# Expert stage of a diffusion step on one core: turns joined, weight rows paired, more buffers, last product reordered

## The chip, the core and the metric

One core of a Trainium2 chip runs the whole program. The metric is the device time of one launch in microseconds, taken several times; the profile is one further execution, recorded by the hardware profiler.

## What is computed

One layer of a hybrid backbone in float32: 128 context tokens and 512 latent tokens, each of 1,024 features. A mixer (a gated linear recurrence and differential attention behind one input projection) is followed by a mixture of 16 experts. Each expert chooses its tokens itself, 64 latent and 16 context ones, so that it always works on 80 rows:

```
aff = softmax(h @ router_w); gate, idx = top_k(aff per expert, cap)      # cap 64 latent, 16 context
xg = h[idx]                                                              # gathered rows
a = silu(xg @ w_gate[e]) * (xg @ w_up[e])
y = (a @ w_down[e]) * gate
x = x + g2 * scatter_add(y at idx)
```

h is the normalised x, scaled and shifted by a modulation that is itself a product of a conditioning vector with w_mod. The three weight matrices of an expert are 1,024 x 1,024 each, 4 MiB; all experts together are 192 MiB, and each is read once.

## The kernel before, in words

There is one instruction stream for each engine, written out by hand. The order of the first part comes from a list STEPS that all engines walk through; the expert stage has loops of its own. Waits are on semaphores.

**Ahead of the experts.** Weights come in pieces of 1 MiB or less through three raw buffers, are split by ACT (L959) and DVE (L1186) into a high and a low part (w_hi, w_lo), and the activations lie split in act_hi and act_lo. The small inputs are loaded by SP at L760 between the pieces, five of them on the semaphore s_late, for which DVE (L1366) and PE (L1812, L1838) wait. After the output projection each token tile is normalised to xn2, written to a DRAM tensor xn_rows (SP, L840), turned by PE with eight transposes (L1982) for the router, and the residual is written to the output (SP, L834). Then DVE picks the tokens of all experts, PE makes the rows of the second modulation (L1725, L1792, L1793), and GpSimd starts the first indirect gather.

**Experts on PE.** The weights of an expert are 12 pieces of 1 MiB (gate 4, up 4, down 4), each two blocks of 128 input features by 1,024 outputs; a piece's two blocks are its two "halves". piece_mm (L2030) takes one piece: for each half it runs four matmuls at L2037 for the latent rows (stationary operand 128 x 32 tokens, moving 512 columns, into four 32-partition strips of one PSUM bank) and four at L2040 for the context rows (256 columns each). The trace lists each float32 matmul as two. The order on PE for expert e is gate(e), up(e), down(e-1). turn_x(e+1) (L2017, L2020) stands in the middle of up(e): eight transposes that bring the 80 gathered rows xg into the layout features by tokens, into PSUM pair 3. turn_a(e) (L2044, L2047) stands at the end: six transposes of the hidden activations aa, into the same pair. The last down product has no other work beside it and is done in the same order, piece by piece (L2089).

**Experts on the other engines.** DVE: xmod (L1645, L1647) scales and shifts the turned tokens into xT; hidden (L1652) multiplies silu(gate) by up; yout (L1661 for the latent rows, L1666 for the context rows) scales the down product into ye. ACT: silu (L1159) and the copy of the turned activations to hT (L1161). GpSimd: an indirect gather (L906) for each expert from xn_rows into the one buffer xg, and two indirect scatters with addition (L922 for the latent rows, L925 for the context rows) into the outputs; at the end of each scatter it waits until both have landed.

**Weights in the expert stage.** SP issues the 192 pieces at L823 into a ring of NRE = 14 buffers. Fourteen pieces come as buffers fall free from the first part: piece 0 early, 1 to 4 when the last projection is done, 5 to 8 around the last rows of the outputs (L841 to L844), 9 and 10 after the first gather has landed (L848), 11 to 13 when the last modulation pieces are used. From then on piece n waits at L853 for PE to be done with piece n - 14. act_hi and act_lo lie idle in the expert stage.

The diff touches these functions:

Of the kernel before, what the change touches and what calls it, by code (L numbers as in the profile page):

```python
# [39 lines left out]
def fused_step(nc, A, outs):  # L40
# [8 lines left out]
    with ExitStack() as ctx:  # L49
# [169 lines left out]
        NRE, NP = 14, 12 * NE  # L219
# [12 lines left out]
        Wraw = [[ctx.enter_context(nc.sbuf_tensor(f"w_raw{v}{s}", [P, 2048], F32))[:, :] for s in range(NHL)] for v in range(2)]  # L232
        brow = arena[:, o_vso + 2048:o_vso + 2560]
# [11 lines left out]
        xpsum = pair(3).rearrange("p (k t) -> p k t", k=KD)[:, :, 0:CAP]  # L245
# [374 lines left out]
        s_silu, s_a, s_aT, s_ahi, s_y, s_yc, s_scat = (sem(n) for n in ("s_silu", "s_a", "s_aT", "s_ahi", "s_y", "s_yc", "s_scat"))  # L620
# [13 lines left out]
        eraw = [Wraw[1][last_w[0]]] + [Wraw[v][s] for s in last_w[1:] for v in range(2)] + eraw_x  # L634
# [92 lines left out]
        def _(sp):  # L727
# [30 lines left out]

            def load_small(dst, src, sig):
                sp.dma_start(dst, src).then_inc(sig, 16)  # L760
# [16 lines left out]
            for dst, src in small[2:]:  # L777
                load_small(dst, src, s_late)
            STORES = {("gl", 3): range(0, 4), ("gl", 4): range(4, 8), ("f", 0): range(8, 12), ("q", 0): range(12, 16), ("gl", 5): range(16, 20),
                      ("mod", 6, 0): (20, 21), ("mod", 6, 1): (22, 23), ("mod", 7, 0): (24, 25, 26), ("gl", 7): (27,), ("mod", 4, 0): range(28, 32)}  # L780
            out_at = {"nk": RAWNO[("tok", 3, 1)], "nv": RAWNO[("tok", 4, 1)]}
            for n in range(9, len(PIECES)):
# [23 lines left out]
                if n == RAWNO[("out", 1, 0)]:  # L806
# [4 lines left out]
                    sp.dma_start(router, A["router_w"][0].rearrange("(k p) e -> p k e", p=P)).then_inc(s_x1in, 16)  # L811
            wg, wu, wd = (A[n][0] for n in ("w_exp_gate", "w_exp_up", "w_exp_down"))

            def epiece(n):
# [7 lines left out]
                src = w[ex, 2 * P * k:2 * P * k + 2 * P, :].rearrange("(k p) n -> p k n", p=P)  # L822
                sp.dma_start(eraw[n % NRE].rearrange("p (k n) -> p k n", k=2), src).then_inc(s_er[n % NRE], 16)  # L823
# [39 lines left out]
        def _(pool):  # L863
# [52 lines left out]
            def scatter(e):  # L916
                g.tensor_copy(iscat[0:CAP_LAT, 0:1], iS[0:CAP_LAT, e:e + 1]).then_inc(s_icq, 1)
# [1252 lines left out]
```

## Time and profile before

| | us |
|---|---|
| median of 3 runs | 1274.31 |
| lowest, highest | 1273.91, 1276.9 |
| profiled execution, its own time | 1280.71 |
| its span, first to last instruction | 1278.8 |
| PE busy in the span | 1182.0 |
| DVE, ACT, POOL busy | 569.9, 353.5, 137.2 |

PE is the matmuls, PEld the loads of stationary operands, POOL is GpSimd, SP the engine that issues most DMAs (SPq its queue). Matmuls are pipelined and their ends modelled, so that a busy PE need not be at its peak. Rows of the timeline merge instructions of one line that follow each other closely.

### The profile page before, as it was taken

To read this page: it belongs to the slowest core of one execution; us is meant where nothing else is said; L and a number is where in the kernel's file an instruction comes from. 1 tells how busy PE (TensorE), PEld (TensorE's weight loads), DVE (VectorE), ACT (ScalarE), POOL (GpSimd) and SP (SyncE) were. 2 spreads that over 40 slices of the span, in tenths; PEclk is the share of its full clock that TensorE was granted. 3 is DMA by queue.
4 is the path that set the end of the run, shared out by engine and by line. 5 is a ranking of instruction groups with operands and counts; after the bars stand their busy time and mean duration, and the time that the engine had idled before them with its cause. 6 is when DMAs were issued, how large, how long until landed. Compare 5 with 4: busy or idle time off the path is not lost.

```text
span 1278.8 us, 24225 instructions
## 1 busy us (share of the span) xinstructions
PE 1182.0 (92%) x10653; PEld 776.5 (61%) x10653; DVE 569.9 (45%) x833; ACT 353.5 (28%) x561; POOL 137.2 (11%) x192
## 2 busy tenths in 40 slices
PE   5789999999998979679899799999999999999996
PEld 2577888888888868579777434444444444444442
DVE  2787343656268778888875610111111111111112
ACT  3312324555358577554231210000000000000000
POOL 1022000121000101100001000111111111111001
PEclk7889999999999899979999689999999999999999
DMA  8620630311314212206555899999999999999994
GB/s 317 227 97 2 227 101 16 93 43 60 104 44 121 81 60 100 81 18 261 175 172 214 312 347 393 392 390 390 391 391 392 391 391 391 392 394 392 393 400 128
DMA packets 111904, 296.81 MB, mean 232 GB/s; under 512 B 7092, under 2 KB 33076, under 8 KB 111800
## 3 DMA queue, kind: packets, MB, share of 16 engines
q1 hardware_dynamic: 108280, 284.25, 59.0%
q0 software_dynamic: 3520, 11.01, 3.7%
q8 instruction: 84, 1.38, 0.5%
q14 instruction: 20, 0.16, 0.0%
HBM read 278.47 MB, written 16.78 MB: 231 GB/s over the span
## 4 chain that ended last, share of the span: by engine, by line
PE 47%; DVE 2%; ACT 1%; issue 0%; DMA 0%; POOL 0%; POOLq 0%; DVEq 0%; ACTq 0%
PE ps L2037 26%; PE ps L2040 13%; PE ps L1693 1%; PE ps L1695 1%; PE ps L1694 1%; PE ps L2047 1%; PE ps L2020 1%; DVE arena L1310 1%; PE ps L1725 1%; PE ps L1995 1%; PE ps L1982 0%; DMA arena<-in_w_out_dram 0%; ACT w_hi L959 0%; DVE w_lo L1186 0%; DVE arena L1565 0%
## 5 line engine op out<-in xcount | busy, mean ns | idle before, releaser
L2037 PE MATMUL ps<-arena 128*32 128x512 f32 x1952 | 254.5, 593 | 0.9 <-ACT arena L1161 0.9
L1693 PE MATMUL ps<-act_hi,w_hi 128*128 128x320 f32 x576 | 184.7, 321 | 5.2 <-DVE w_lo L1186 2.1
L1695 PE MATMUL ps<-act_hi,w_lo 128*128 128x320 f32 x576 | 179.5, 312 | 0.0
L1694 PE MATMUL ps<-act_lo,w_hi 128*128 128x320 f32 x576 | 179.5, 312 | 0.0
L2040 PEld LDWEIGHTS ps<-arena 128*32 128x32 f32 x1952 | 63.4, 110 | 146.0 <-issue 146.0
L2040 PE MATMUL ps<-arena 128*32 128x256 f32 x1952 | 150.0, 379 | 0.0
L2037 PE MATMUL ps<-w_raw,arena 128*32 128x512 f32 x1120 | 147.8, 600 | 1.4 <-DVE arena L1678 1.4
L1693 PE MATMUL ps<-w_hi,act_hi 128*128 128x512 f32 x280 | 113.7, 406 | 11.8 <-DVE w_lo L1186 4.9
L1693 PEld LDWEIGHTS ps<-act_hi,w_hi 128*128 128x128 f32 x576 | 109.7, 191 | 8.6 <-issue 2.9
L1695 PE MATMUL ps<-w_hi,act_lo 128*128 128x512 f32 x280 | 110.8, 396 | 0.0
L1694 PE MATMUL ps<-w_lo,act_hi 128*128 128x512 f32 x280 | 110.7, 395 | 0.0
L1694 PEld LDWEIGHTS ps<-act_lo,w_hi 128*128 128x128 f32 x576 | 109.7, 190 | 0.0
L1695 PEld LDWEIGHTS ps<-act_hi,w_lo 128*128 128x128 f32 x576 | 109.7, 190 | 0.0
L1645 DVE TENSOR_TENSOR arena<-ps,arena 128x640 f32<-128x640 f32 x15 | 12.4, 824 | 210.6 <-PE ps L2020 210.6
L1161 ACT ACTIVATE arena<-ps 128x768 f32<-128x768 f32 x16 | 13.0, 810 | 337.1 <-PE ps L2047 337.1
L1186 DVE TENSOR_TENSOR w_lo<-arena,w_hi 128x2048 fp32r<-128x2048 f32 (+1 forms) x34 | 73.6, 2166 | 56.3 <-ACT w_hi L959 55.6
L1661 DVE SCALAR_TENSOR_TENSOR arena<-ps,arena 64x512 f32<-64x512 f32 x32 | 23.9, 748 | 148.4 <-PE ps L2040 148.2
L2040 PEld LDWEIGHTS ps<-w_raw,arena 128*32 128x32 f32 x1120 | 36.5, 111 | 85.4 <-issue 85.4
L2037 PEld LDWEIGHTS ps<-arena 128*32 128x32 f32 x1952 | 61.5, 110 | 42.1 <-issue 1.5
L2040 PE MATMUL ps<-w_raw,arena 128*32 128x256 f32 x1120 | 86.7, 382 | 0.0
L963 ACT ACTIVATE arena<-ps 128x512 f32<-128x512 f32 (+2 forms) x80 | 48.4, 617 | 111.4 <-PE ps L1832 27.8
L959 ACT ACTIVATE w_hi<-arena 128x2048 fp32r<-128x2048 f32 (+1 forms) x34 | 61.3, 1808 | 53.4 <-PE ps L1695 24.6
(221 smaller groups left out, 1464.4 us busy)
## 6 DMA issues: line engine op xcount, KB each, us to landing
arena<-in_w_exp_up_dram SPq DMA_DIRECT2D x41, 1024.0 KB
arena<-in_w_exp_down_dram SPq DMA_DIRECT2D x41, 1024.0 KB
arena<-in_w_exp_gate_dram SPq DMA_DIRECT2D x40, 1024.0 KB
w_raw<-in_w_exp_gate_dram SPq DMA_DIRECT2D x24, 1024.0 KB
w_raw<-in_w_exp_up_dram SPq DMA_DIRECT2D x23, 1024.0 KB
w_raw<-in_w_exp_down_dram SPq DMA_DIRECT2D x23, 1024.0 KB
arena<-in_w_mod_dram SPq DMA_DIRECT2D x22, 1024.0 KB, 5.3
arena<-in_w_in_dram SPq DMA_DIRECT2D x18, 1024.0 KB, 6.4
```

Of the source, the lines that this page charges most:

```text
L959: a.activation(hl(key)[0][:, 0:w], rawv(key)[:, 0:w], ACT.Copy).then_inc(s_hi, 1)
L963: release(a.activation(dst, src, func, **kw), key)
L1161: a.activation(hT, pair(3)[:, 0:HW], ACT.Copy).then_inc(s_ahi, 1)
L1186: v.tensor_tensor(l_[:, 0:w], rawv(key)[:, 0:w], h_[:, 0:w].bitcast(F32), ALU.subtract).then_inc(s_lo, 1)
L1310: ins = v.scalar_tensor_tensor(out=out, in0=w[:, kk, :], scalar=by, in1=out, op0=ALU.mult, op1=ALU.add)
L1661: ins = v.scalar_tensor_tensor(out=ye[lat, to], in0=y[64 * b:64 * b + 64, 0:512], scalar=gT[lat, e:e + 1], in1=G2[lat, to], op0=ALU.mult, ...
L1693: t.matmul(out, sh, mh, start=start, stop=False)
L1694: t.matmul(out, sh, ml, start=False, stop=False)
L1695: return t.matmul(out, sl, mh, start=False, stop=stop)
L1725: ins = t.matmul(bank(2 * modpair(j))[32 * kk:32 * kk + 32, :], cond_row[:, 2 * kt:2 * kt + 32], w[:, kk, :], start=s == 0, stop=s == 1)
L2037: t.matmul(bank(2 * pr)[32 * s:32 * s + 32, :], lat[:, 32 * (s % 2):32 * (s % 2) + 32], w[:, kk, 512 * (s // 2):512 * (s // 2) + 512], sta ...
L2040: ins = t.matmul(bank(2 * pr + 1)[32 * s:32 * s + 32, 0:256], ctx_, w[:, kk, 256 * s:256 * s + 256], start=kt == 0, stop=kt == 7)
```

## The change

Five edits come together. The tokens of expert e+2 are turned directly behind the activations of expert e, into PSUM pair 1 (from e = 1 on; the first three turns stay where they were), and the gathers are issued one expert further ahead. The weight pieces are read with two neighbouring rows of the matrix in each partition, so that one partition reads 8,192 bytes in one run; everything that meets those weights follows that order of features: the transposes of x, a and xn2 take every second column, the modulation columns of the second half and their small inputs are paired too, the latter by eight loads of single elements at the start. The ring has 19 buffers, the five new ones (Araw) in the room of act_hi and act_lo, and SP's first pieces are issued in another order. The last down product does the latent rows of all four pieces first, then the context rows. DVE works off yout before the xmod of the expert after next.

```diff
-        NRE, NP = 14, 12 * NE
+        NRE, NP = 19, 12 * NE
+        Araw = [ctx.enter_context(nc.sbuf_tensor(f"a_raw{s}", [P, 2048], F32))[:, :] for s in range(2 * KD * T // 2048)]
-        xpsum = pair(3).rearrange("p (k t) -> p k t", k=KD)[:, :, 0:CAP]
+        def xpair(e):
+            return 3 if e < 3 else 1
+        def xpsum(e):
+            return pair(xpair(e)).rearrange("p (k t) -> p k t", k=KD)[:, :, 0:CAP]
+        def paired(k):
+            return slice(2 * P * (k // 2) + k % 2, 2 * P * (k // 2) + 2 * P, 2)
...
-        eraw = [Wraw[1][last_w[0]]] + [Wraw[v][s] for s in last_w[1:] for v in range(2)] + eraw_x
+        eraw = [Wraw[1][last_w[0]]] + [Wraw[v][s] for s in last_w[1:] for v in range(2)] + Araw + eraw_x
...
 # SP
+            def load_second():
+                sp.wait_ge(s_small, 32)
+                c = A["cols"].rearrange("(p k) n -> p k n", k=2)
+                for h, r in enumerate(HALF):
+                    for dst, c0, n in ((n2c, 8, 8), (bcol[:, 24:40], 56, 16)):
+                        for k in range(2):
+                            with nc.allow_non_contiguous_dma("pairs of features"):
+                                sp.dma_start(dst[r, k::2], c[:, k, c0 + h:c0 + n:2]).then_inc(s_late, 16)
...
             for dst, src in small[2:]:
                 load_small(dst, src, s_late)
+            load_second()
...
-                src = w[ex, 2 * P * k:2 * P * k + 2 * P, :].rearrange("(k p) n -> p k n", p=P)
-                sp.dma_start(eraw[n % NRE].rearrange("p (k n) -> p k n", k=2), src).then_inc(s_er[n % NRE], 16)
+                src = w[ex, 2 * P * k:2 * P * k + 2 * P, :].rearrange("(p k) n -> p (k n)", k=2)
+                sp.dma_start(eraw[n % NRE], src).then_inc(s_er[n % NRE], 16)
...
-            epiece(5)
+            for n in range(5, 11):
+                epiece(n)
             sp.wait_ge(s_yrow, 16 * NT)
-            for n in range(6, 9):
+            sp.wait_ge(s_gath, 16)
+            for n in range(11, 14):
                 epiece(n)
             sp.wait_ge(s_sq2, NT)
             filled(sp, ("logits", 1))
             filled(sp, ("affT", 1))
-            sp.wait_ge(s_gath, 16)
-            epiece(9)
-            epiece(10)
+            epiece(14)
+            epiece(15)
             for n, key in enumerate(LAST_MOD):
                 sp.wait_ge(*used[key])
-                epiece(11 + n)
+                epiece(16 + n)
...
 # GpSimd
             def scatter(e):
+                if e:
+                    pool.wait_ge(s_scat, 32 * e)
...
-                if e + 1 < NE:
-                    pool.wait_ge(s_scat, 32 * e + 32)
             fetch(iT)
-            gather(1)
-            gather(2)
+            for e in range(1, 4):
+                gather(e)
             pool.wait_ge(s_gt, 5)
-            for e in range(2, NE - 1):
-                gather(e + 1)
-                scatter(e - 2)
-            for e in range(NE - 3, NE):
+            for e in range(NE):
+                if e + 4 < NE:
+                    gather(e + 4)
                 scatter(e)
...
 # DVE
-                dve.wait_ge(s_eu, down_made(e))
+                if e + 1 < NE:
+                    dve.wait_ge(s_eu, down_made(e))
+                else:
+                    dve.wait_ge(s_dl, 1)
...
                 ins.then_inc(s_y, 1)
+                if e + 1 == NE:
+                    dve.wait_ge(s_eu, down_made(e))
...
-            for e in range(NE):
-                if e + 1 < NE:
-                    xmod(e + 1)
+            xmod(1)
+            hidden(0)
+            xmod(2)
+            for e in range(1, NE):
                 hidden(e)
-                if e:
-                    yout(e - 1)
+                yout(e - 1)
+                if e + 2 < NE:
+                    xmod(e + 2)
...
 # PE
-                        ins = t.transpose(pair(USE[st][0])[:, P * q:P * q + P], xn2[q_ % 2][:, P * q:P * q + P], ident)
+                        ins = t.transpose(pair(USE[st][0])[:, P * q:P * q + P], xn2[q_ % 2][:, paired(q)], ident)
...
-                    ins = t.transpose(pair(3)[:, P * q:P * q + CAP], xg[0:CAP, P * q:P * q + P], ident[0:CAP, 0:CAP])
+                    ins = t.transpose(pair(xpair(e))[:, P * q:P * q + CAP], xg[0:CAP, paired(q)], ident[0:CAP, 0:CAP])
...
+            def last_down():
+                w = []
+                for kt in range(8):
+                    if kt % 2 == 0:
+                        w.append(arrived(NP - 4 + kt // 2))
+                    ins = latents(0, of_h(hT, kt)[0], w[kt // 2], kt)
+                ins.then_inc(s_dl, 1)
+                for kt in range(8):
+                    ins = context(0, of_h(hT, kt)[1], w[kt // 2], kt)
+                    if kt % 2:
+                        ins.then_inc(s_eu, 1)
...
-                    ins = t.transpose(pair(3)[:, P * q:P * q + P], aa[:, P * q:P * q + P], ident)
+                    ins = t.transpose(pair(3)[:, P * q:P * q + P], aa[:, paired(q)], ident)
...
                     if j == 4:
                         pe.wait_ge(s_a, e)
-                    if j == 6 and e + 1 < NE:
-                        pe.wait_ge(s_ahi, e)
-                        turn_x(e + 1)
+                        if e >= 2 and e + 1 < NE:
+                            pe.wait_ge(s_xgm, e + 2)
+                    if j == 6 and e == 1:
+                        pe.wait_ge(s_ahi, 1)
+                        turn_x(2)
...
-                if e + 1 < NE:
-                    pe.wait_ge(s_xgm, e + 2)
+                if e == 1:
+                    pe.wait_ge(s_xgm, 3)
                 turn_a(e)
+                if e + 2 < NE:
+                    turn_x(e + 2)
             pe.wait_ge(s_ahi, NE)
-            for q in range(4):
-                piece_mm(NP - 4 + q, 0, of_h, hT, q)
+            last_down()
```

latents and context are the two loops of piece_mm, taken apart; arrived(n) is its wait for piece n.

## Rows read from the trace of the kernel before

**Rows 1.** The page's 40 slices of the span: GB/s that the DMA moved.
```profile
GB/s 317 227 97 2 227 101 16 93 43 60 104 44 121 81 60 100 81 18 261 175 172 214 312 347 393 392 390 390 391 391 392 391 391 391 392 394 392 393 400 128
```

**Rows 2.** Windows: stretch, length, busy us per engine, granted clock, DMA share, GB/s.
```profile
740.00:746.90 6.90, 5.50 (x38) 1.95 (x40) 2.03 (x6) 1.68 (x2) 1.28 (x2) 0.51 0.98 386
765.60:1256.60 491.00, 491.00 (x5977) 202.69 (x5967) 86.37 (x129) 24.31 (x30) 63.32 (x84) 1.00 1.02 390
```

**Rows 3.** Waits of the weight loader, 765.6 to 1250: us in total, times, longest.
```profile
PEld ps L2040 <- issue: 212.4, 710, 0.3
```

**Rows 4.** DMA from 900 to 932.75: packets, MB, share; a gather's us to landing.
```profile
q1 hardware_dynamic: 3141, 12.12, 93.7%
...
arena<-xn_rows,arena POOLq DMA_INDIRECT x1, 7.7
```

**Rows 5.** DMA from 1262 to 1270, the only queue with packets.
```profile
q0 software_dynamic: 81, 0.20, 15.4%
```

**Rows 6.** Timeline from 1256 to the end: start, length, engine, line.
```profile
1258.09 1.06 PE L2037 MATMUL ps<-arena 128*32 128x512 f32 x8 [0.90 <-ACT arena L1161]
...
1265.86 1.04 PE L2037 MATMUL ps<-arena 128*32 128x512 f32 x8
...
1268.69 1.51 DVE L1661 SCALAR_TENSOR_TENSOR arena<-ps,arena 64x512 f32<-64x512 f32 x2 [8.73 <-PE ps L2040]
1270.23 1.97 DVE L1666 SCALAR_TENSOR_TENSOR arena<-ps,arena 16x256 f32<-16x256 f32 x4
1270.99 1.44 POOL L922 DMA_INDIRECT out_dram<-arena  x1 [6.38 <-DVE arena L1661]
1272.73 1.29 POOL L925 DMA_INDIRECT out_dram<-arena  x1 [0.30 <-issue]
```

**Rows 7.** Timeline around a turn of x and a turn of a.
```profile
912.00 1.04 PE L2037 MATMUL ps<-arena 128*32 128x512 f32 x8
912.86 0.61 PE L2040 MATMUL ps<-arena 128*32 128x256 f32 x8
913.41 0.62 PEld L2020 LDWEIGHTS ps<-arena 80*128 80x128 f32 x8 [0.41 <-issue]
...
914.11 1.06 PE L2037 MATMUL ps<-arena 128*32 128x512 f32 x8
...
929.18 0.61 PE L2040 MATMUL ps<-arena 128*32 128x256 f32 x8
...
930.53 1.07 PE L2037 MATMUL ps<-arena 128*32 128x512 f32 x8
```

**Rows 8.** Line L2020: ns shortest/median/longest of one load.
```profile
L2020 PEld LDWEIGHTS ps<-arena x128: 137/140/226, 739.6 to 1208.6; 80*128 80x128 f32 x128
```

**Rows 9.** Timeline at the start of the expert stage.
```profile
734.09 1.09 POOL L906 DMA_INDIRECT arena<-xn_rows,arena  x1 [22.18 <-DVE arena L1629]
...
738.49 1.39 SPq L823 DMA_DIRECT2D arena<-in_w_exp_gate_dram  x3
...
739.63 1.00 PE L2020 MATMUL ps<-arena 80*128 80x80 f32 x8
```

**Rows 10.** DMA from 730, 740, 42.8, 645 (2.2 us each of these two), 38.
```profile
arena<-xn_rows,arena POOLq DMA_INDIRECT x1, 4.3
...
arena<-xn_rows,arena POOLq DMA_INDIRECT x1, 8.9
...
q1 hardware_dynamic: 211, 0.93, 102.7%
...
q1 hardware_dynamic: 1105, 0.26, 54.1%
...
arena<-in_w_in_dram SPq DMA_DIRECT2D x1, 1024.0 KB, 11.2
```

**Rows 11.** Timeline of SP and ACT, 41 to 58.
```profile
41.70 0.45 SPq L749 DMA_DIRECT2D arena<-in_w_in_dram  x1
...
57.99 1.90 ACT L959 ACTIVATE w_hi<-arena 128x2048 fp32r<-128x2048 f32 x1
```

More of the change, by code:

```diff
@@ L619, in fused_step @@
         s_icp, s_gath, s_xgT, s_xgf = (sem(n) for n in ("s_icp", "s_gath", "s_xgT", "s_xgf"))
-        s_silu, s_a, s_aT, s_ahi, s_y, s_yc, s_scat = (sem(n) for n in ("s_silu", "s_a", "s_aT", "s_ahi", "s_y", "s_yc", "s_scat"))
+        s_silu, s_a, s_aT, s_ahi, s_dl, s_y, s_yc, s_scat = (
+            sem(n) for n in ("s_silu", "s_a", "s_aT", "s_ahi", "s_dl", "s_y", "s_yc", "s_scat"))
         def gate_made(e):
@@ L1704, in turn_row @@
                 for q in range(4):
-                    ins = t.matmul(bank(2 * colpair(j) + 1)[:, 2 * q:2 * q + 2], mrow_of(j)[:, P * q:P * q + P], pick, start=True, stop=True)
+                    ins = t.matmul(bank(2 * colpair(j) + 1)[:, 2 * q:2 * q + 2], mrow_of(j)[:, paired(q) if j >= 6 else slice(P * q, P * q + P)], pick,
+                                   start=True, stop=True)
                 wrote(ins, ("modcol", j))
@@ L1816, in _ @@
                         for c in range(2):
-                            ins = t.matmul(bank(5)[:, 2 * q + c:2 * q + c + 1], wsum[9][:, c, P * q:P * q + P], reset[:, 1:2], start=True, stop=True)
+                            ins = t.matmul(bank(5)[:, 2 * q + c:2 * q + c + 1], wsum[9][:, c, paired(q)], reset[:, 1:2], start=True, stop=True)
                     wrote(ins, ("modcol", 9))
@@ L2028, in of_h, with arrived, latents @@
                 return w[:, lat:lat + 64], w[:, ctx_:ctx_ + 32]
+            def arrived(n):
+                pe.wait_ge(s_er[n % NRE], 16 * (n // NRE + 1))
+                return eraw[n % NRE].rearrange("p (k n) -> p k n", k=2)
+            def latents(pr, x, w, kt):
+                for s in range(4):
+                    ins = t.matmul(bank(2 * pr)[32 * s:32 * s + 32, :], x[:, 32 * (s % 2):32 * (s % 2) + 32],
+                                   w[:, kt % 2, 512 * (s // 2):512 * (s // 2) + 512], start=kt == 0, stop=kt == 7)
+                return ins
@@ L2030, in piece_mm, with context @@
+            def context(pr, x, w, kt):
+                for s in range(4):
+                    ins = t.matmul(bank(2 * pr + 1)[32 * s:32 * s + 32, 0:256], x,
+                                   w[:, kt % 2, 256 * s:256 * s + 256], start=kt == 0, stop=kt == 7)
+                return ins
             def piece_mm(n, pr, of, src, j):
-                pe.wait_ge(s_er[n % NRE], 16 * (n // NRE + 1))
-                w = eraw[n % NRE].rearrange("p (k n) -> p k n", k=2)
-                for kk in range(2):
-                    kt = 2 * j + kk
+                w = arrived(n)
+                for kt in range(2 * j, 2 * j + 2):
@@ L2035, in piece_mm @@
                     lat, ctx_ = of(src, kt)
-                    for s in range(4):
-                        t.matmul(bank(2 * pr)[32 * s:32 * s + 32, :], lat[:, 32 * (s % 2):32 * (s % 2) + 32],
-                                 w[:, kk, 512 * (s // 2):512 * (s // 2) + 512], start=kt == 0, stop=kt == 7)
-                    for s in range(4):
-                        ins = t.matmul(bank(2 * pr + 1)[32 * s:32 * s + 32, 0:256], ctx_,
-                                       w[:, kk, 256 * s:256 * s + 256], start=kt == 0, stop=kt == 7)
@@ L2042, in piece_mm @@
-                ins.then_inc(s_eu, 1)
+                    latents(pr, lat, w, kt)
+                    ins = context(pr, ctx_, w, kt)
+                ins.then_inc(s_eu, 1)
+            def last_down():
[9 more added lines that the diff above has]
+                        ins.then_inc(s_eu, 1)
```

12 lines of the change are left out of this document (6 added, 6 removed).

## The prediction, made before the changed kernel had run

> **What bounds the kernel now.** I read the page's 40 slices first, then windows, waits and the timeline of the expert stage. The slices show two kernels in one: up to slice 23 (735 us) the DMA comes and goes, from there it moves about 390 GB/s until one slice before the end [rows 1]. That is the expert stage, and the chain of waits lies there on PE's two product lines, L2037 and L2040.
>
> PE or DMA? Both are full: in the 491 us from 765.6 PE is busy 491.00, the DMA share is 1.02 [rows 2]. The waits decide. Of that stretch the answer for PE's matmuls is empty and the weight loader's idle is all "issue", four lines like the one shown [rows 3]: PE waits for nobody and sets the pace. The DMA is slightly slower than PE, though. An expert is 24 half pieces of 1.29 us, one turn of x (0.82) and one of a (0.92, both below), 32.7 us. A stretch of that length moves 12.12 MB on the weights' queue [rows 4], and PE uses twelve pieces of 1,048,576 bytes, 12.58 MB. So the weights' lead shrinks by 0.44 piece, 1.2 us, an expert. It is never used up: after 1262 all 81 packets are POOL's [rows 5], and the last piece is first used at 1265.86 [rows 6]. Buffers and bandwidth bound nothing, by some 4 us at the end.
>
> **Turning x behind turning a.** Within a half piece four 512-column products take 0.86 us (912.00 to 912.86); the six halves from 1258.09 to 1265.86 give 1.29 us each, so 0.43 is left for the four of 256 columns [rows 6, 7]. Across turn_x, 912.86 to 914.11 less 0.43, eight transposes cost 0.82 us; across turn_a, 929.18 to 930.53 less 0.43, six cost 0.92 [rows 7]. The eight loads of turn_x span 0.62 us and last 140 ns each, so one follows another every (620 - 140) / 7 = 69 ns, 0.55 us in all [rows 7, 8]. The other 0.27 us are the way from 32-column tiles to the whole array and back. Behind turn_a it is not paid again: 0.27 us less for each of the experts 3 to 15, 13 x 0.27 = 3.5. I take 3.5, the row's own difference. Bounds: 0 (the second block pays its own entry) and 13 x 0.41, all of the loader's idle before a turn [rows 7], 5.3. It is PE's own time, nothing covers it. What could be late next: DVE frees up's PSUM for xmod after yout's 1.5 + 2.0 us [rows 6] and two short operations, and PE wants it at j = 4, four pieces or 10.3 us on. gather(e+4) is issued in front of scatter(e) on POOL, a period ahead of its turn, and takes 7.7 us [rows 4]; gather(3) has half a period. The scatter's wait for the scatter before, moved to its front, has a period too. All 0.
>
> **Last down product.** From 1258.09 eight latent groups of 0.86 end at 1264.95, eight context groups of 0.43 at 1268.4, as now. DVE's latent part and its scatter's issue move beside PE. The context part starts at 1268.69 in place of 1270.23, takes 1.97, and POOL issues its scatter 0.79 later (as 1270.20 to 1270.99): at 1271.45 instead of 1272.73 [rows 6]. It lands last, so the end comes 1.3 us sooner; bounds 0 and 1.54. The last piece is needed six latent groups in, at 1263.25, and was there by 1262.
>
> **Nineteen buffers.** SP now issues pieces 5 to 10 in one go at 713, and 11 to 18 behind the first gather; until now the queue ran empty and piece 9 was issued at 738.49 [rows 9]. The lead grows by a piece or two, worth 0, as PE waits for none. It costs something at the gather. gather(0), issued at 734.09 into a queue nearly empty, took 4.3 us; gather(1), with five pieces queued, 8.9; one of the steady stage 7.7 [rows 4, 9, 10]. With 9 and 10 queued as well, the first is of the latter kind: 734.09 + 7.7 = 741.8, and turn_x(0), at 739.63 now [rows 9], starts 2.2 us later with all expert products behind it. I take +2.2. Bounds: 0 (now 1.2 us of slack, and few packets before it) and 734.09 + 8.9 - 739.63 = 3.4. The clock adds to this: granted 0.51 over 740.0 to 746.9, mostly its 1.2 GHz level, after DVE's top-k had PE idle in part, and 1.00 over the 491 us [rows 2]. Two half pieces run at half speed, 1.29 us each lost. A late start may have one fewer or one more: 0, bounds -1.3 and +1.3.
>
> **Rows paired.** A partition's piece is one run of 8,192 bytes in place of two of 4,096. No weight load before has that length. The nearest: 42.8 to 45 us, mostly constants of 6,144 and 3,584 bytes, 0.93 MB in 2.2 us at share 1.027, 411 GB/s for a full DMA; the steady stage, 12.12 MB in 32.75 us at 0.937, 395 [rows 4, 10]. Longer runs are rather 4% faster; worth 0, bounds in rival 3. The Trainium skill ("DMA: Bandwidth & Descriptors", SWDGE vs HWDGE vs iDMA) wants packets of at most 4,096 bytes, because the engine changes queues at packet borders; by that rule a gather beside these loads waits up to twice as long for its turns, some 4 us more. No trace here shows it.
>
> **Strided transposes.** To match, x, a and xn2 are turned with every second column as stationary operand, which no row shows. Lower bound 0: the loads overlap, two at a time. Upper: a load of 280 ns, still two at a time, gives a pace of 140: 71 ns more for each of x's; a's moving side has 128 columns, not 80, its pace now by the same rate 69 x 128 / 80 = 110, so 30 more. 8 x 71 + 6 x 30 = 0.75 us, x 15 = 11.2, and 40 of xn2 at 30 ns, 1.2: 12.4. I take 0, the row's pace [rows 8]. The skill ("Advanced Engine Details and Errata", SBUF Cachelines) says that reads run at full speed with at least two hits on a 16-byte line. A step of two fp32 makes exactly two; by it the cost is 0, at the very edge.
>
> **Eight small loads at the start.** 3,072 elements of 4 bytes each. SP's issues there take some 0.5 us, 4 us for eight, ahead of the load now issued at 41.70. A stretch of 64-byte router rows gives 0.541 x 2.2 us x 16 / 1105 = 17 ns a packet; 3,200 of them with their signals over 16 engines, 3.4 us of DMA [rows 10]. The piece behind them landed 11.2 us after 41.70, at 52.9; ACT, busy till then, reads it at 57.99 [rows 10, 11]: 5.1 us hide it, since the issues run beside a full queue. 0, bounds 0 and 3. The paired modulation columns and the router load: a few short instructions, 0.
>
> **Sum.** -3.5 - 1.3 + 2.2 = -2.6. The profiled execution, span 1278.8, time 1280.71, becomes 1278.1; it stands 6.4 above the median of the runs, and the difference is the same there: 1274.31 - 2.6 = 1271.7.
>
> **Rivals.**
> 1. The gather isn't late: its packets take turns with the weights' and few are before it. -3.5 - 1.3 = -4.8, 1269.5. For: the slack of 1.2 us. Against: both gathers beside a full queue took over 7.5.
> 2. The strided load shows: 12.4 - 2.6 = +9.8, 1284.1, slower. It decides from 3.8 + 2.6 = 6.4 us, 0.43 an expert, at a pace of about 115 ns for x's transposes in place of 69. For: a load already lasts twice its pace, so any more shows at once. Against: no row.
> 3. Paired rows are slower by 3% of the 490 us, 15 us; the lead covers some 5, PE waits 10: 1282. It decides beyond 2%. Against: 411 over 395.
> 4. The start is worse: gather 3.4, small loads 3, clock 1.3, half the merge: +7.7 - 3.1 = +4.6, 1278.9, slower.
> 5. The merge saves nothing (operand rows change from 128 to 80): -1.3 + 2.2 = +0.9, 1275.2, the same.
>
> **How the numbers follow.** A measurement of this kernel tells 0.3%, 3.8 us, from no change. Forecast 0.46 (0.08 of it at the fast edge), rival 1 0.26, rival 2 0.12, rival 3 0.04, rival 4 0.06, rival 5 0.06. Faster 0.26 + 0.08 = 0.34, same 0.38 + 0.06 = 0.44, slower 0.22. The forecast's own range is 1268.8 to 1275.5. For 8 in 10 it reaches down through rival 1 to 1268 and up through rival 4 but not rival 2, to 1281.
>
> **What would show it.** In the changed kernel's profile: L2020's transposes right behind L2047's, and 32.5 us from one turn to the next; x's transposes 69 ns apart (else rival 2); gather(0) landing near 7.7 us after its issue and the first turn near 742; no PE wait for a DMA; the last scatter issued 2.8 us after PE's last product rather than 4.1. I am wrong if PE waits for a weight piece, if the pace of the transposes changes, or if the stages before 700 us move by over 1 us.

## The result: 0.65% slower, and the profile after

Timed side by side, the changed kernel takes 1282.97 us (median of 5 runs, 1281.59 to 1287.03) and the kernel before 1275.38 (5 runs, 1273.91 to 1277.8): a ratio of 1.0065, 95% interval 1.0043 to 1.0088. I had forecast 1271.7 and a range from 1268 to 1281. Both the time and the side were wrong.

The profiled execution (1282.78 us, at the median of its kernel) has a span of 1280.9 us, 2.1 over that of before, whose profiled execution lay above its own median. So the traces are compared stage by stage, by the distance between events (where xn2's turn falls, 681.6 us here and 683.7 before, varies by itself from 680.4 to 684.6 over the traces of this study).

The stage first. Windows of the changed kernel (columns as in [rows 2]): PE is as full as it was, at the same granted clock, and the answer for PE's waits from 765.6 to 1256.6 is empty here too.
```profile
740.00:746.90 6.90, 5.50 (x35) 1.96 (x37) 2.03 (x6) 0.00 (x0) 1.27 (x2) 0.50 0.95 360
765.60:1256.60 491.00, 491.00 (x5938) 209.97 (x5933) 86.22 (x128) 24.34 (x30) 60.19 (x84) 1.00 0.99 387
```
PE waits for nobody, yet from the start of the first expert matmul to the start of the last the stage takes 529.96 us (742.21 to 1272.17) where it took 526.20 (742.03 to 1268.24). The waits can't explain that; PE's own work got longer. The weight loader shows it: it is busy 209.97 us in place of 202.69. One line's loads, ns shortest/median/longest, as [rows 8], the turn of x and then the turn of a:
```profile
L2047 PEld LDWEIGHTS ps<-arena x128: 195/223/226, 739.5 to 1196.7; 80*128 80x128 f32 x128
...
L2096 PEld LDWEIGHTS ps<-arena x96: 195/209/219, 771.9 to 1260.7; 128*128 128x128 f32 x96
```
A load of x takes 223 ns where it took 140. The timeline around a joined pair of turns (as [rows 7]):
```profile
931.17 0.61 PE L2069 MATMUL ps<-arena 128*32 128x256 f32 x8
...
931.72 0.79 PEld L2096 LDWEIGHTS ps<-arena 128*128 128x128 f32 x6 [0.41 <-issue]
...
932.42 1.05 PEld L2047 LDWEIGHTS ps<-arena 80*128 80x128 f32 x8
...
933.55 0.16 PEld L2063 LDWEIGHTS ps<-arena 128*32 128x32 f32 x8
```
The turn of x does stand right behind that of a, as forecast. But its eight loads span 1.05 us, not 0.62, which is (1050 - 223) / 7 = 118 ns apart. From 931.17 to the products at 933.55, less the 0.43 of the context group, the pair takes 1.95 us; apart and contiguous the two took 0.82 + 0.92 = 1.74.

The start (as [rows 9]): the first gather, issued at 731.07, frees PE at 739.50, 8.4 us later where it was 5.5. PE has waited 2.8 us for it.
```profile
731.07 1.09 POOL L926 DMA_INDIRECT arena<-xn_rows,arena  x1 [20.90 <-DVE arena L1648]
...
739.43 0.33 SPq L842 DMA_DIRECT2D arena<-in_w_exp_gate_dram  x1
...
739.50 1.31 PE L2047 MATMUL ps<-arena 80*128 80x80 f32 x8 [2.81 <-DMA arena<-xn_rows,arena]
```
The granted clock is 0.50 from 737.0, in that wait, to 747.2; before it was 0.50 from 740.0 to 746.9. So the first turn of x runs wholly at the low level, and from its start to the first product are 2.71 us, before 2.40.

The kernel before has a delay of its own here, which its trace shows and most others don't. A product of the second modulation stands ahead of the small ones that bring the gather's indices. It falls into a stretch of granted clock 0.50 (719.6 to 736.6) and takes 2.00 us; in the changed kernel the clock is at 1.00 there (726.8 to 730.2) and it takes 1.09:
```profile
729.32 2.00 PE L1792 MATMUL ps<-arena 128*80 128x512 f32 x2 [0.78 <-ACT arena L963]
```
```profile
727.61 1.09 PE L1819 MATMUL ps<-arena 128*80 128x512 f32 x2 [0.78 <-ACT arena L982]
```
From the turn of xn2 to the gather's issue are 50.4 us in that trace and 49.5 in the changed kernel's, although the changed one spends 0.4 more on the turns of xn2. In ten of the thirteen traces of this study it is 49.0 to 49.1, or 49.5 with the strided turns. So the comparison at the start favours the changed kernel by 1.3 us.

The steady stage's DMA, 900 to 932.75 (as [rows 4]): 1,702 packets for 12.40 MB, where 3,141 carried 12.12 MB.
```profile
q1 hardware_dynamic: 1702, 12.40, 92.9%
...
arena<-xn_rows,arena POOLq DMA_INDIRECT x1, 9.3
```
The end (as [rows 6]):
```profile
1262.02 3.64 PE L2063 MATMUL ps<-arena 128*32 128x512 f32 x32 [0.90 <-ACT arena L1180]
...
1270.64 1.91 PE L2069 MATMUL ps<-w_raw,arena 128*32 128x256 f32 x32
...
1271.46 1.44 POOL L944 DMA_INDIRECT out_dram<-arena  x1 [2.19 <-DVE arena L1683]
1272.79 1.96 DVE L1690 SCALAR_TENSOR_TENSOR arena<-ps,arena 16x256 f32<-16x256 f32 x4 [2.12 <-PE ps L2069]
1275.04 1.29 POOL L947 DMA_INDIRECT out_dram<-arena  x1 [2.13 <-DVE arena L1690]
```
The last scatter is issued 2.87 us after PE's last context product starts (1272.17); before it was 4.49. From that start to the end of the span are 8.7 us, before 10.6.

The small loads (as [rows 11]): eight issues occupy SyncE for 8.4 us, twice what I had reckoned, and the first load of the input projection leaves at 49.92 in place of 41.70. ScalarE reads it at 57.75, before at 57.99. The third piece of the projection lands at 61.49, before at 58.20, and ScalarE, free 0.07 us earlier, takes it at 61.51. The small loads cost next to nothing, but the cover was used up.
```profile
41.50 8.38 SPq L775 DMA_DIRECT2D arena<-cols_dram  x8
...
49.92 1.72 SPq L758 DMA_DIRECT2D arena<-in_w_in_dram  x3
...
57.75 5.68 ACT L978 ACTIVATE w_hi<-arena 128x2048 fp32r<-128x2048 f32 x3
```

### The profile page after: what moved, and what is told of

Same layout as the page of the kernel before. It is cut to its first block, busy times and chain, and to the rows that moved or that the text cites. A ratio compares the mean times of both kernels' runs of the same rounds, so it can differ in the third digit from the quotient of the medians.

```text
span 1280.9 us, 24195 instructions
## 1 busy us (share of the span) xinstructions
PE 1182.0 (92%) x10653; PEld 784.1 (61%) x10653; DVE 569.9 (44%) x833; ACT 353.6 (28%) x561; POOL 134.1 (10%) x192
## 4 chain that ended last, share of the span: by engine, by line
PE 46%; DVE 3%; DMA 1%; ACT 1%; issue 1%; POOL 0%; POOLq 0%; DVEq 0%; ACTq 0%
PE ps L2063 26%; PE ps L2069 13%; PE ps L1719 1%; PE ps L1721 1%; PE ps L1720 1%; PE ps L2047 1%; PE ps L2096 1%; DMA arena<-xn_rows,arena 1%; DVE arena L1329 1%; PE ps L2022 1%; PE ps L2009 0%; DMA arena<-in_w_out_dram 0%; DVE w_lo L1205 0%; ACT w_hi L978 0%; DVE arena L1580 0%
## 5 line engine op out<-in xcount | busy, mean ns | idle before, releaser
L2063 PE MATMUL ps<-arena 128*32 128x512 f32 x1440 | 187.1, 593 | 0.9 <-ACT arena L1180 0.9
L1671 DVE TENSOR_TENSOR arena<-arena,ps 128x768 f32<-128x768 f32 x16 | 15.3, 954 | 252.6 <-PE ps L2069 252.6
L2069 PEld LDWEIGHTS ps<-arena 128*32 128x32 f32 x1440 | 46.8, 110 | 106.4 <-issue 105.9
L2063 PE MATMUL ps<-w_raw,arena 128*32 128x512 f32 x832 | 109.5, 602 | 1.4 <-DVE arena L1702 1.4
L2069 PE MATMUL ps<-arena 128*32 128x256 f32 x1440 | 110.1, 379 | 0.0
L2063 PE MATMUL ps<-a_raw,arena 128*32 128x512 f32 x800 | 104.2, 593 | 0.0
L1719 PEld LDWEIGHTS ps<-w_hi,act_hi 128*128 128x128 f32 x280 | 53.1, 190 | 29.5 <-issue 5.9
L2063 PEld LDWEIGHTS ps<-arena 128*32 128x32 f32 x1440 | 45.9, 110 | 32.4 <-issue 1.8
```

The costliest lines, as they stand in the source:

```text
L1671: v.tensor_tensor(aa[:, 0:HW], aa[:, 0:HW], pair(1)[:, 0:HW], ALU.mult).then_inc(s_a, 1)
L1719: t.matmul(out, sh, mh, start=start, stop=False)
L2063: ins = t.matmul(bank(2 * pr)[32 * s:32 * s + 32, :], x[:, 32 * (s % 2):32 * (s % 2) + 32], w[:, kt % 2, 512 * (s // 2):512 * (s // 2) + 5 ...
L2069: ins = t.matmul(bank(2 * pr + 1)[32 * s:32 * s + 32, 0:256], x, w[:, kt % 2, 256 * s:256 * s + 256], start=kt == 0, stop=kt == 7)
```

## Experiments

The theory: a step of two in what TensorE loads as stationary operand costs it, on PE's own path, and everything else in the change came out about as forecast. The rivals: the paired rows or the longer queue cost; the joined turns save nothing; the late start is the whole of it. All ratios are to the kernel before, run beside the experiment on the same chip.

**The step taken out of the changed kernel.** Transposes load contiguous columns, the weight rows stay paired, so features don't match rows.
```diff
-ins = t.transpose(pair(xpair(e))[...], xg[0:CAP, paired(q)], ...)
+ins = t.transpose(pair(xpair(e))[...], xg[0:CAP, P * q:P * q + P], ...)
 (the same for aa and xn2)
```


> The changed kernel with the three kinds of turns (x, a, xn2) read contiguously again; weights stay paired, so features and weight rows don't match and the output isn't the reference's. Theory S (the step of two in the stationary operand sets the transposes' pace): in the changed kernel's trace transposes of x and a alike follow each other every 120 ns, before 69 and 109. Contiguous they go back: a merged turn takes 1.47 us instead of 1.95, the three single turns of x 0.82 instead of 1.22, of a 0.92 instead of 1.03, xn2's eight 1.07 instead of 1.19. 13 x 0.48 + 3 x 0.40 + 3 x 0.11 + 0.6 = 8.4 us less than the changed kernel, so about 0.8 us under the kernel before (ratio 0.999). Rival P (paired rows, the ring or the order of DMAs cost the time): no faster than the changed kernel, ratio 1.006, with the turns' pace gone back all the same. Gather(0) stays late in both: about 7.5 us to landing.

Measured: 1277.1 us, ratio 0.9989 (0.9976 to 1.0002). Its timeline around the joined turns:
```profile
931.61 0.61 PE L2069 MATMUL ps<-arena 128*32 128x256 f32 x8
...
932.15 0.64 PEld L2096 LDWEIGHTS ps<-arena 128*128 128x128 f32 x6 [0.41 <-issue]
...
932.76 0.67 PEld L2047 LDWEIGHTS ps<-arena 80*128 80x128 f32 x8
...
933.51 0.16 PEld L2063 LDWEIGHTS ps<-arena 128*32 128x32 f32 x8
```
933.51 - 931.61 - 0.43 = 1.47 us for the pair: 0.27 under 1.74, exactly the merge term, and 0.48 under the strided pair. The stage is 522.44, 7.5 under the changed kernel. Its first gather was the slowest of all (9.2 us; PE waited 4.1), so the time shows less than the stage does.

**The step alone put into the kernel before** (features again don't match rows).
```diff
-ins = t.transpose(pair(3)[...], xg[0:CAP, P * q:P * q + P], ...)
+ins = t.transpose(pair(3)[...], xg[0:CAP, paired(q)], ...)
 (the same for aa and xn2)
```


> The kernel before with nothing changed but that x, a and xn2 are turned with every second column as stationary operand; the output isn't the reference's, since the weights stay as they were. Theory S: transposes every 120 ns, a turn of x 1.22 us, of a 1.03, so an expert period of 33.2 us instead of 32.7, 16 x 0.40 + 16 x 0.11 + 0.6 = 8.8 us slower than before, ratio 1.007. Rival P: the pace seen in the changed kernel comes from the joined turns or from the other traffic into the buffers, then x stays at 69 ns here and the time is that of before. If the load lead matters at all, it gets larger here, as PE is slower.

Measured: 1287.57 us, ratio 1.0073 (1.0054 to 1.0092), the stage 533.85 against 526.20. One line's loads:
```profile
L2023 PEld LDWEIGHTS ps<-arena x128: 194/218/226, 737.8 to 1214.4; 80*128 80x128 f32 x128
```
The turn of x takes 0.40 us more, that of a 0.11: 15 x 0.40 + 16 x 0.11 = 7.8, and 7.65 were seen. Taken out or put in, the step is worth 7.5 to 7.7 us of the stage (7.4 and 8.0 without the first four half pieces, by the table at the end of this section). The theory stands.

**What a step costs in general**: in the changed kernel xn2 was read with a step of eight, a with three, x with four.
```diff
-ins = t.transpose(pair(xpair(e))[...], xg[0:CAP, paired(q)], ...)
+ins = t.transpose(pair(xpair(e))[...], xg[0:CAP, 4 * P * (q // 4) + q % 4:4 * P * (q // 4) + 4 * P:4], ...)
 (aa: step 3; xn2: step 8)
```


> The changed kernel with other steps in what the transposes load as stationary operand: xn2 with a step of eight fp32, a with three, x with four (so which feature meets which row is changed). Known so far: step one 69 ns (x, 80 columns moving) and 110 (128 columns moving), step two 120 for both. If every element apart from its neighbour is read by itself, the pace is 120 for any step from two on. If the load is read in lines of 16 bytes, it grows to four and stays: 180 for three, 240 for four and for eight. If it goes by the span that is read, 480 for eight. One look: joined turns 6 x 0.18 + 8 x 0.24 = 3.0 us if it goes by the line, stage 529.96 + 15 x 1.2 = 548.

A single run, 1286.06 us, so only its trace is used: stage 529.60. Its loads:
```profile
L2047 PEld LDWEIGHTS ps<-arena x128: 196/217/231, 743.1 to 1200.0; 80*128 80x128 f32 x128
...
L2096 PEld LDWEIGHTS ps<-arena x96: 190/202/217, 775.5 to 1264.0; 128*128 128x128 f32 x96
```
The transposes come 120 ns apart at a step of four, 117 at three, 111 at eight (at one 69 with 80 columns moving, 109 with 128). Each step was tried on another tensor, so each is compared with the same tensor at a step of two, where all three have 120: nothing grows with the step, and two is already the full price. Neither a line of 16 bytes nor the span that is read fits; each element read by itself would, but that is a reading of the pace and not shown.

**All pairing taken out of the changed kernel**: rows of 4,096 bytes, contiguous transposes, no small loads. The joined turns, the nineteen buffers, SyncE's order and the last product stay.
```diff
-src = w[ex, ...].rearrange("(p k) n -> p (k n)", k=2)
+src = w[ex, ...].rearrange("(k p) n -> p k n", p=P)
-                load_small(...); load_second()
+                load_small(...)
 (transposes as in the first experiment; modulation columns and router as before)
```


> The changed kernel with everything of the pairing taken out: weight rows of 4,096 bytes, contiguous turns, no eight small loads, modulation columns as before. Merged turns, 19 buffers, SP's new order and the last product's new order stay. Theory S: same as the kernel with plain turns within 1 us, ratio 0.999 to before; the expert stage (first to last product) 521.5 us against 526.2 before and 530.0 changed. The lead of the weights at the end falls from about 20 us to 4 or 5 but PE waits for none. Rival P: paired rows themselves cost, then this one is faster than the one with plain turns by some us. Rival L (the eight small loads and the paired columns cost early on): stages before 700 us shorter by over 1 us.

Measured: 1276.13, ratio 0.9981 (0.9967 to 0.9996). The stage is 521.62; the first gather takes 7.3 us and PE waits 2.0 for it. The profiled execution, 1271.78 us, is the shortest of its twelve. Two of the rivals fall here. With or without long rows the joined, contiguous kernel takes the same time (0.9989 with, 0.9981 without, the intervals overlap), so the paired rows don't cost the 8 us. And the small loads don't: the turn of xn2 comes at 680.4 here, but over all traces at 680.4 to 683.7 without them and at 681.4 to 684.6 with them. The means differ by 0.8 us, so a cost of about 1 us is not excluded.

This run also shows that rows of 4,096 bytes can carry the joined turns. PE waits for no piece, but it is close: the last piece has 1.2 us of slack.

**The same with pieces 9 and 10 queued behind the first gather.**
```diff
-for n in range(5, 11): epiece(n)
+for n in range(5, 9): epiece(n)
 sp.wait_ge(s_yrow, 16 * NT)
 sp.wait_ge(s_gath, 16)
-for n in range(11, 14): epiece(n)
+for n in range(9, 14): epiece(n)
```


> As the unpaired kernel, but SP issues pieces 9 and 10 behind the first gather's landing like the rest, 5 to 8 before it. Theory G (the weights queued ahead make the first gather late): gather(0) lands 4.3 us after its issue, the wait of PE before the first turn goes, 2.2 to 2.9 us less than the unpaired kernel, ratio to before 0.9965. Rival: the gather's time doesn't depend on the two pieces, or the time is lost again at the granted clock: within 1 us of the unpaired kernel. With it the lead of the weights falls by a piece, no wait.

Measured: 1276.13, ratio 0.9982 (0.997 to 0.9993). The gather lands in 5.9 us and the first product comes 1.8 us sooner after the turn of xn2 (57.3 for 59.1). Against what I expected, PE then waits for weights near the end, at pieces 157, 183, 187 and 191, 2.8 us in all; the stage is 525.42. The median is that of the run before, so the gain is lost again. That it is the same to the digit is chance. The longest of them:
```profile
1169.53 1.06 PE L2062 MATMUL ps<-a_raw,arena 128*32 128x512 f32 x8 [0.92 <-DMA a_raw<-in_w_exp_up_dram]
```

**The joined turns alone** on the kernel before: fourteen buffers, 4,096-byte rows, its queue order and last product.
```diff
+if j == 4 and e >= 2 and e + 1 < NE: pe.wait_ge(s_xgm, e + 2)
-if j == 6 and e + 1 < NE:
-    pe.wait_ge(s_ahi, e); turn_x(e + 1)
 turn_a(e)
+if e + 2 < NE: turn_x(e + 2)
 (with it PSUM pair 1, GpSimd's gathers one expert earlier and DVE's order, as in the changed kernel)
```


> The kernel before with the turn of x joined to the turn of a alone: fourteen buffers, rows of 4,096 bytes, contiguous transposes, SyncE's order and the last product as before. Theory (a joined pair of turns pays the 0.27 us between tile shapes once, and nothing else comes): pair of turns 1.47 us instead of 0.82 + 0.92, 13 x 0.27 = 3.5 us less in the stage, the end weights' slack shrinks from 5.3 and 3.3 us to between 0 and 2, so PE waits at most 1 us for them: stage 522.7 to 523.7, ratio to the kernel before 0.9970 to 0.9985. Rival (without more buffers the joined turns gain nothing, since the DMA sets the end): PE waits 2 to 3.5 us for the last pieces, stage 525 to 526, ratio 0.999 to 1.000; then the nineteen buffers or the long rows are what lets the merge pay.

Measured: 1277.52, ratio 0.9994 (0.9982 to 1.0005), stage 525.25. The rival was right. The slack of a piece (landing to first use) falls from 23.2 us at piece 16 to 0.4 at 168 and 0.0 at 157, 183 and 187, and PE waits. Its waits, 760 to 1275 (us in total, times, longest):
```profile
PE ps L2055 <- DMA w_raw<-in_w_exp_up_dram: 1.2, 2, 0.9
...
PE ps L2055 <- DMA arena<-in_w_exp_down_dram: 0.4, 1, 0.4
```
The half pieces at these three points start 1.0, 0.5 and 0.6 us late, 2.2 us together. From the fifth half piece on, the merge brings 1.4 us of the 3.7 that it brings where no weights are waited for: DMA, as near a second bound as [rows 4] said, takes the rest. It had less to lose than the trace of before shows. In that trace the slack at piece 183 is 3.3 us. The kernel with the last product alone (below) has the same expert stage up to there, and its trace has 2.1.

**The long rows alone** in the kernel before (features don't match rows).
```diff
-src = w[ex, ...].rearrange("(k p) n -> p k n", p=P)
+src = w[ex, ...].rearrange("(p k) n -> p (k n)", k=2)
```


> The kernel before with each expert weight piece as one run of 8,192 bytes per partition and nothing else, the transposes contiguous (so rows and features don't match; only the weights' loads are changed). Theory (the long rows make the DMA 3 to 4% faster but PE sets the pace): packets of 8,192 bytes at 312 ns in place of 4,096 at 161, the last piece's slack 12 to 20 us instead of 5.3, expert stage 526 to 526.5 as before, ratio 0.999 to 1.001. Rival (long packets hold up the gathers so that a turn waits): gather(0) over 6 us and a wait of PE for the gather within the experts, ratio over 1.002.

Measured: 1280.4, ratio 1.0025 (1.0011 to 1.0038), outside what I expected and inside the rival's range. The last piece's slack is 13.3 us in place of 5.3, the stage 525.99 against 526.20. The DMA from 765.6 to 1200, of this kernel and then of the one before, shows what changed in the stage:
```profile
q1 hardware_dynamic: 22473, 163.64, 92.7%
...
arena<-xn_rows,arena POOLq DMA_INDIRECT x13, 9.2
```
```profile
q1 hardware_dynamic: 41641, 160.54, 93.8%
...
arena<-xn_rows,arena POOLq DMA_INDIRECT x13, 8.4
```
2% more bytes at a smaller share. The 3.2 us aren't in its trace. The first gather is over 6 us, as the rival said (6.4 against 4.3, PE waits 2.6), but PE waits for no later one, and from the turn of xn2 to the first product are 58.2 us, before 58.3. Two other kernels with this queue order and short rows, the joined turns alone and the last product alone, have 56.6 and 56.7, so up to 1.6 us may lie at the start. With one trace each that is not shown. Its runs had a mean granted clock of 0.963 against 0.965 for those of before beside it, which at the slope among the latter (0.4 us per 0.001) is 1 us. The rest is open. The kernels with joined turns don't repeat it: with all rows paired and contiguous transposes (below) the ratio is 0.9975, with none paired 0.9981.

**The last product alone** in the kernel before.
```diff
-for q in range(4):
-    piece_mm(NP - 4 + q, 0, of_h, hT, q)
+last_down()
 (with it DVE's wait for s_dl ahead of its latent part)
```

> The kernel before with the last down product's latents first and nothing else. Theory: DVE's latent part and its scatter's issue go beside PE, the last scatter is issued 2.8 us after PE's last product instead of 4.5, the tail behind the last product is 8.7 to 8.8 us instead of 10.6, and the last piece, wanted 3.9 us in place of 7.8 us after the product's start minus its own share, is still there in time or up to 1 us late: time 1 to 1.9 us less, ratio 0.9985 to 0.9993. Rival (the last weight piece is not there): PE waits in the latents' groups, and the gain is under 0.5 us.

Measured: 1277.1, ratio 0.9996 (0.9983 to 1.0008). In the trace the theory's numbers come out: the last scatter 2.7 us after PE's last product starts, 8.5 us from there to the end, 2.0 less than before, and no wait for the last piece. The ratio allows for it but doesn't prove it: it was expected at 0.9985 to 0.9993.

**The version with the pairs taken apart by the writers.** The whole result, with rows paired and transposes contiguous: whoever writes xn2 and a reads with a step of two.
```diff
+def evenodd(w): return w.rearrange("p (b k q) -> p b k q", k=2, q=P)
+def by_pairs(w): return w.rearrange("p (b q k) -> p b k q", k=2, q=P)
-a.activation(aa[:, 0:HW], pair(0)[:, 0:HW], ACT.Silu)
+a.activation(evenodd(aa[:, 0:HW]), by_pairs(pair(0)[:, 0:HW]), ACT.Silu)
 (the same for DVE's norm into xn2 and for the product silu(g) * u)
```


> The changed kernel with its result whole, but the pairs are taken apart by whoever writes the row (the norm's write of xn2, ScalarE's silu and VectorE's product read with a step of two and write in order), so that all transposes load contiguous columns. Theory (the step of two costs in TensorE's load only): transposes 69/110/110 ns apart as in the kernel before, the joined turns 1.47 us instead of 1.95, expert stage 522 to 523 us instead of 530, time 5 to 8 us below the changed kernel, ratio to the kernel before 0.996 to 1.000; silu stays near 812 ns and the product near 954, and if they grow nobody waits, since 10 us lie between silu and j = 4. Rival (a step of two costs any reader, and ScalarE's or VectorE's longer read comes on the path): silu and product 1.6 to 1.9 us, and a wait of PE for s_silu before each expert's first piece, 15 x 0.5 to 0.8 us, stage 530 again, ratio 1.004 or more.

Measured: 1276.01, ratio 0.9975 (0.9965 to 0.9986), stage 522.80. The writers, mean ns of one:
```profile
L1184 ACT ACTIVATE arena<-ps 128x768 f32<-128x768 f32 x15 | 12.2, 811 | 147.2 <-PE ps L2075 147.2
```
```profile
L1677 DVE TENSOR_TENSOR arena<-arena,ps 128x768 f32<-128x768 f32 x16 | 15.3, 954 | 246.3 <-PE ps L2075 246.3
```
811 and 954 ns: in the changed kernel the same operations without a step took 812 and 954. VectorE's write of xn2, which reads x with the step, takes 753 to 756 ns and took 752 to 753. The same step that takes the pace of TensorE's loads from 69 to 120 ns costs these two engines nothing, from PSUM at that.

**That version with pieces 9 and 10 behind the first gather** (edit as above).

> As the run before, with weight pieces 9 and 10 queued behind the first gather instead of in front of it. Theory (gather(0) waits among the weights' packets queued in front of it): it lands in 5.5 to 6.5 us instead of 7.5 to 9, the first turn is 1.5 to 3 us earlier, and as the 8,192-byte rows leave a lead of over 12 us, no wait for weights comes in its place (it did with rows of 4,096 bytes): time 1 to 3 us below the run before, ratio to the kernel before 0.994 to 0.998. Rival (the gather's time is set by the packets already under way or by the clock at the start, not by pieces 9 and 10): within 1 us of the run before.

Measured: 1273.57, ratio 0.9964 (0.9951 to 0.9976), the lowest ratio of all, though its interval overlaps that of the version before it (0.9965 to 0.9986). The gather takes 5.2 us and PE goes from the modulation's last product to the turn without waiting; the least slack of a piece is just under 6 us, at piece 160.
```profile
732.03 1.09 POOL L932 DMA_INDIRECT arena<-xn_rows,arena  x1 [20.88 <-DVE arena L1654]
...
737.29 0.33 SPq L848 DMA_DIRECT2D a_raw<-in_w_exp_gate_dram  x1
...
737.37 0.75 PE L2053 MATMUL ps<-arena 80*128 80x80 f32 x8
```

**The same on fourteen buffers**, with SyncE's order of the kernel before.
```diff
-NRE = 19
+NRE = 14
-eraw = [...] + Araw + eraw_x
+eraw = [...] + eraw_x
```


> The version with pairs taken apart by the writers, on fourteen buffers and with SyncE's order of the kernel before, so joined turns, long rows and the last product's order are kept and only the nineteen buffers and the early pieces are out. Theory (the long rows alone give the lead that the joined turns need, the extra buffers give nothing): no wait of PE for a weight piece, stage 522.8 to 523.3, gather(0) 5 to 6 us as pieces 9 and 10 come behind it, ratio to the kernel before 0.995 to 0.9975, like the best so far. Rival (buffers are needed: with fourteen the lead is spent as it was with rows of 4,096 bytes): PE waits 2 us or more for weights near the end, stage 525 or more, ratio 0.998 to 1.000.

Measured: 1274.47, ratio 0.9971 (0.9958 to 0.9985), stage 522.43, no wait for a piece; the last one has 8.0 us of slack, the least is 7.6 at piece 161. Not to be told from the run before. Beside long rows the five buffers give nothing. Beside short rows it depends on the queue: nineteen buffers with pieces 9 and 10 ahead of the gather let the joined turns pay in full, nineteen with the two behind it don't, and neither do fourteen.

**The stages side by side.** A stage's first four half pieces run partly at a granted clock of 0.50, and how many of them do so varies; from the fifth on it is 1.00 in every trace. The table splits the stage there (us).

| kernel | first four half pieces | the rest |
|---|---|---|
| before; long rows alone; last product alone | 7.56; 7.35; 7.85 | 518.65; 518.65; 518.64 |
| before, with the step | 7.24 | 526.62 |
| changed kernel; with steps three, four, eight | 7.67; 7.64 | 522.29; 521.96 |
| changed, contiguous turns; writers split; the same, gather first; the same, fourteen buffers | 7.50; 7.86; 8.02; 7.49 | 514.94; 514.94; 514.95; 514.94 |
| unpaired; unpaired, gather first | 6.68; 7.69 | 514.94; 517.74 |
| joined turns alone | 8.01 | 517.23 |

Every kernel with joined, contiguous turns and no wait for weights has the same 514.94, 3.7 under the kernel before. The step adds 7.4 to the joined kernel (15 turns of x and 16 of a, 13 of them in pairs) and 8.0 to the kernel before. Where PE waited for weights, 2.3 and 2.8 us are missing.

## Why the prediction was wrong

**The step that failed is the strided transposes at 0.** I had the right bounds (0 to 12.4 us, pace up to 140 ns) and the right mechanism as rival 2, and took the lower end, the pace of the row. But those loads had been contiguous; the row said nothing on a step. What it did say, I had written down in that rival: a load lasts twice its pace, so any longer load shows at once. It came out at 120 ns for x, a and xn2, for x 0.72 of the way from 69 to 140. Term by term: 13 joined pairs x 0.48 + 2 turns of x x 0.40 + 3 of a x 0.11 = 7.4 us of the stage (the first experiment: 7.5), and 40 x 11 ns = 0.4 at xn2, 7.8 in all. Rival 2 set its point of decision at about 115 ns, and with 120 it decided. I gave it 0.12. That its time, 1284.1, lies near the measured 1282.97 is luck: it was made with a term of 12.4.

What tipped me was the Trainium skill ("Advanced Engine Details and Errata", SBUF Cachelines): two hits on a 16-byte line suffice for full speed. For TensorE's stationary operand in fp32 the runs contradict it: two hits (a step of two, 120 ns apart) already cost the whole price, one hit (steps four and eight, 120 and 111) no more. I had called it "the very edge", and an edge that no row shows is a coin toss, not a 0.12.

**Turning x behind turning a: right in size, 0.27 us a pair.** The stage without the step was 522.44, and 526.20 - 3.5 = 522.7; past the first four half pieces 3.7 us were saved. What I missed is that the saving has a condition. I said of the lead that it is never used up, though it shrinks by 1.2 us an expert; the merge takes another 0.27 an expert, 3.5 in all, from a slack that at its least was 2.6 (piece 169) and at the end 5.3. With the kernel before's buffers, rows and queue order 2.3 us are lost to that. It went unpunished in the changed kernel, whose rows are long and whose pieces 9 and 10 come early; either was enough in the experiments (the early pieces with nineteen buffers).

**Last down product: 1.3 forecast, 1.87 seen.** I took the 0.79 us between DVE's end and GpSimd's issue from the latent part [rows 6]. Behind the context part it is 0.3 (1274.75 to 1275.04), though DVE started 0.2 later after PE's last product than I had reckoned. Another 0.2 is gained behind the issue.

**Nineteen buffers and the gather: right in kind, and the number partly by luck.** From the turn of xn2 (683.7 before, 681.6 after) to the first product it was 58.3 and is 60.6 us, +2.3 for my +2.2. But from the gather's issue to the turn of x it is +2.9 (8.4 for 5.5), the low clock in that turn adds 0.3 and the strided turns of xn2 0.4, and the 1.3 us that the kernel before lost ahead of its gather in that one execution hide as much. Over the traces, gather(0) took 7.3, 8.0, 8.1, 8.3 and 9.2 us with pieces 9 and 10 in front of it, and 4.2 to 6.4 in the eight with them behind it, on fourteen buffers or nineteen. The first four half pieces took 0.1 us more.

**Paired rows: right.** 8,192 bytes take 312 ns (median), two packets of 4,096 took 2 x 162; the last piece's slack went from 5.3 to 20.3 us. The Trainium skill's rule on packets over 4,096 bytes ("DMA: Bandwidth & Descriptors", SWDGE vs HWDGE vs iDMA) had some truth, in size too small to matter: gathers of the joined kernels take 7.3 to 7.4 us beside short rows and 8.3 to 8.8 beside long ones, 1 us and not 4, and PE waits for none but the first.

**Small loads: 0.07 us in the trace for my 0,** though the issues took 8.4 us, not 4. I had the cover of the first piece behind them right (5.1 us and a full queue) and the size wrong; the third piece came 3.3 us later than before and was just in time.

**The sum.** From the turn of xn2 to the end the two traces differ by +2.3 + 3.8 - 1.9 = +4.2 us (start, stage, end). By terms: the step 7.8, the merge -3.7, the last product -1.9, the gather 2.9, the clock 0.4, and -1.3 for the delay in the execution of before. Without that delay it is +5.5, where I had -2.6: of the 8.1 between, 7.8 are the term taken as 0. The measured ratio is +8.3 us (5.5 to 11.2), so the terms reach its lower end, and up to some 3 us at its middle aren't located. The long rows alone also came out dearer in time than in their trace, but the joined kernels with long rows didn't.

## What to carry to other kernels

Where a layout change puts a step into somebody's reads, ask whose: TensorE's stationary operand paid for every step that was tried in fp32 (two, three, four, eight), while ScalarE and VectorE that write the tensor anyway took it for nothing here. A saving on PE is worth no more than the least slack of the weights in the stage, so set the one against the other before you count it, and take the slack from more than one trace (3.3 and 2.1 us at the same piece here). And look at the granted clock on both sides before you take the difference of two traces: one slow stretch ahead of a gather was worth 1.3 us. And price a step that no row shows between its bounds, above all if the nearest row says that nothing hides it.

## What the runs showed of the hardware

- fp32 stationary operand, 128 columns: contiguous 140 ns a load, 69 ns apart; step two, three, four or eight 193 to 223 ns a load, 111 to 120 apart (128 moving columns alone give 109).
- ScalarE's 128x768 silu and VectorE's product, reading PSUM with a step of two and writing in order: 811 and 954 ns, as without.
- A DMA packet of 8,192 bytes takes 312 ns, one of 4,096 took 162 (medians).
- Eight DMAs of 1 and 2 KB in 4-byte elements held SyncE for 8.4 us, 1.05 each, where the large regular load of [rows 11] took 0.45.
- A gather of 80 rows behind two more queued weight pieces: 7.4 to 9.3 us from its issue to PE's turn of x in five traces; without them 5.3 to 6.6 in eight.
